# A staged transformer kernel on one core: three seams reordered (opening transposes, expert queries, closing stage)

## The reference

```python
h = x @ w_in                                   # projections of 256 tokens
...
x = _layernorm(DEEPNORM_ALPHA * x + (o * jax.nn.silu(gate)) @ w_out, ln_g[i], ln_b[i])
```

```python
x = x + gate1[:, None, :] * (merged @ w_out[l])
h2 = modulate(x, norm_ffn_g[l], shift2, scale2)
# peer_ffn: queries, two sets of 128 sub-keys, top 16 of 256 pairs, then two tables of 16384 rows
q = (hf @ w_q).reshape(T, PEER_HEADS, 2, PEER_HALF)
s = jnp.einsum('thpd,hpnd->thpn', q, sub_keys)
a = jax.nn.gelu(jnp.einsum('cd,chkd->chk', x_c, u), approximate=False)
y = jnp.einsum('chk,chkd->cd', g_c * a, vv)
x = x + gate2[:, None, :] * y
return rmsnorm(x, norm_final_g)
```

## Time and profile before

| | us |
|---|---|
| median of three runs | 1747.11 |
| the profiled execution | 1730.18 |
| its span, first to last instruction | 1728.4 |
| TensorE busy in it | 1615.2 |
| VectorE busy | 1180.4 |
| ScalarE busy | 865.2 |

### The profile page before, as it was taken

How to read it: one execution, slowest core, us unless ns; L and a number is a source line. 1 busy time by engine, 2 the same in 40 slices (tenths; PEclk the granted TensorE clock), 3 DMA queues, 4 the chain that set the end, 5 groups by cost and what they waited for, 6 DMA issues and landing times.

```text
span 1728.4 us, 31280 instructions
## 1 busy us (share of the span) xinstructions
PE 1615.2 (93%) x10766; PEld 1392.1 (81%) x10766; DVE 1180.4 (68%) x2504; ACT 865.2 (50%) x1391; POOL 81.1 (5%) x110
## 2 busy tenths in 40 slices
PE   5889999998998889998999999899999999999996
PEld 4667877896677667776899999899999777778885
DVE  3565656755576666546347999788787999975554
ACT  3564544444556644453235666655655444445553
POOL 1030101100111210000000000000000000000000
PEclk9999989999998989999689999999999999999998
DMA  6544544555555447534244455544444454566552
GB/s 219 174 147 146 195 147 134 189 172 182 175 194 190 163 141 246 164 102 146 97 145 133 162 193 168 172 159 157 157 158 146 159 167 160 166 207 193 192 192 81
DMA packets 77188, 284.83 MB, mean 165 GB/s; under 512 B 9376, under 2 KB 9408, under 8 KB 75840
## 3 DMA queue, kind: packets, MB, share of 16 engines
q1 hardware_dynamic: 73296, 266.95, 46.5%
q0 software_dynamic: 3824, 16.99, 2.9%
HBM read 281.77 MB, written 2.14 MB: 164 GB/s over the span
## 4 chain that ended last, share of the span: by engine, by line
PE 74%; DVE 16%; ACT 4%; issue 3%; DMA 3%; DVEq 0%; SPq 0%; POOL 0%; ACTq 0%
PE banks L639 21%; PE banks L641 20%; PE banks L640 20%; DVE w_lo L1372 5%; PE banks L1027 3%; PE banks L774 2%; DMA raw<-stream 2%; PE banks L811 2%; PE banks L729 2%; PE banks L751 1%; DMA arena<-x_spill 1%; PE banks L823 1%; PE banks L822 1%; DVE arena L1841 1%; ACT w_hi L1085 1%
## 5 line engine op out<-in xcount | busy, mean ns | idle before, releaser
L1372 DVE TENSOR_TENSOR w_lo<-raw,w_hi 128x1024 fp32r<-128x1024 f32 x456 | 558.4, 1229 | 343.1 <-ACT w_hi L1085 338.5
L1085 ACT ACTIVATE w_hi<-raw 128x1024 fp32r<-128x1024 f32 x456 | 481.7, 1058 | 520.2 <-PE banks L641 478.5
L639 PE MATMUL banks<-w_hi,xT_hi 128*128 128x512 f32 (+1 forms) x1140 | 453.8, 398 | 14.9 <-DVE xT_lo L1406 6.0
L641 PE MATMUL banks<-w_hi,xT_lo 128*128 128x512 f32 (+1 forms) x1140 | 442.8, 388 | 0.0
L640 PE MATMUL banks<-w_lo,xT_hi 128*128 128x512 f32 (+1 forms) x1140 | 442.6, 388 | 0.0
L639 PE MATMUL banks<-xT_hi,w_hi 128*128 128x256 f32 (+1 forms) x1392 | 409.2, 294 | 4.9 <-DVE xT_lo L1406 2.9
L640 PE MATMUL banks<-xT_lo,w_hi 128*128 128x256 f32 (+1 forms) x1392 | 403.6, 290 | 0.0
L641 PE MATMUL banks<-xT_hi,w_lo 128*128 128x256 f32 (+1 forms) x1392 | 403.5, 290 | 0.0
L639 PEld LDWEIGHTS banks<-xT_hi,w_hi 128*128 128x128 f32 x1392 | 277.4, 199 | 6.0 <-DVE xT_lo L1406 3.1
L640 PEld LDWEIGHTS banks<-xT_lo,w_hi 128*128 128x128 f32 x1392 | 277.4, 199 | 0.1
L641 PEld LDWEIGHTS banks<-xT_hi,w_lo 128*128 128x128 f32 x1392 | 277.0, 199 | 0.0
(11 more groups left out here) (189 smaller groups left out, 1445.8 us busy)
## 6 DMA issues: line engine op xcount, KB each, us to landing
raw<-stream SPq DMA_DIRECT2D x504, 512.0 KB, 3.6
arena<-ln_in POOLq DMA_DIRECT2D x4, 1024.0 KB, 5.3
arena<-x_spill POOLq DMA_DIRECT2D x3, 1024.0 KB, 10.9
arena<-mod_rows POOLq DMA_DIRECT2D x2, 1536.0 KB, 9.7
arena<-g_in POOLq DMA_DIRECT2D x3, 512.0 KB, 10.6
arena<-x_in SPq DMA_DIRECT2D x2, 512.0 KB, 4.0
arena<-bands_in POOLq DMA_DIRECT2D x1, 1024.0 KB, 6.7
arena<-keys_in POOLq DMA_DIRECT2D x1, 1024.0 KB, 6.1
```

The costliest lines, as they stand in the source:

```text
L639: pe.matmul(out, stationary[0], moving[0], start=first, stop=False, **k)
L641: return pe.matmul(out, stationary[1], moving[0], start=False, stop=last, **k)
L1085: act.activation(w_hi[:, s], half_raw(s), ACT.Copy).then_inc(piece_hi, 1)
L1372: dve.tensor_tensor(w_lo[:, s], half_raw(s), w_hi[:, s].bitcast(F32), ALU.subtract).then_inc(piece_lo, 1)
```

## The change

It has four parts. At the opening, the turned halves don't wait for one another's banks, ScalarE and VectorE evacuate them ahead of the four splits, and TensorE turns both blocks before the first product. The form of the product that takes a feature unit one block at a time goes away. The expert queries wait for both blocks and go through `project` from the first unit on; VectorE modulates block 1 one split earlier and evacuates its turned halves one split earlier. At the end, the last four pieces are multiplied for block 0 first and then for block 1, and each engine closes one block at a time, with the table for the root loaded ahead.

```diff
-                    after = (earlier[half],) if earlier else (closing[0],) if closing else ()
+                    after = (earlier[half],) if earlier else (closing[0],) if closing else (None,)
...
-            def project_opening(unit, turned, turn_other):
+            def project_opening(unit, turned, turn_other=None):
...
-                        if b == 0 and n == RING - 1:
+                        if b == 0 and n == RING - 1 and turn_other is not None:
                             turn_other()
...
-                turn_block(0)
-                project_opening(unit, turned, lambda: turn_block(1))
+                for b in range(B):
+                    turn_block(b)
+                project_opening(unit, turned)
...
-            open_layer(E["q"][0], E["hT"], h_half, 4, peer["h"])
-            for u in E["q"][1:]:
+            for n, u in enumerate(E["hT"]):
+                pe.wait_ge(h_half, 4 + n + 1)
+                turn(u, peer["h"])
+            wait_put(pe, E["hT"])
+            for u in E["q"]:
                 project(u)
...
-            with pe.Fori(0, HALF // RING) as i:
+            with pe.Fori(0, HALF // RING - 1) as i:
                 for s in range(RING):
                     second_table(RING * i + HALF, s)
+            for b in range(B):
+                for s in range(RING):
+                    if b == 0:
+                        pe.wait_ge(piece_lo, n_pieces - RING + s + 1)
+                        pe.wait_ge(hidden_lo, NKEYS - RING + s + 1)
+                    for d in range(D // COLS):
+                        mm = parts_product(banks[:, 2 * b + d], [x[:, s, b * P:(b + 1) * P] for x in (xT_hi, xT_lo)],
+                                           [x[:, s, d * COLS:(d + 1) * COLS] for x in (w_hi, w_lo)],
+                                           False, False, skip_group_check=True)
+                    if b:
+                        mm.then_inc(piece_used, 1)
+                if b == 0:
+                    mm.then_inc(first_block, 1)
...
                 if l == 0:
-                    split_ahead(0)
                     for u in L["xT"]:
                         evacuate_only(u)
+                    split_ahead(0)
...
-            act.wait_ge(x_ready, 2)
+            root_table()
             for b in range(B):
+                act.wait_ge(end_ready, b + 1)
                 link(act.activation(y_end[:, b], x_end[:, b], ACT.Square, accum_out=small[:, 8 + b:9 + b]))
-            act.activation(small[:, 0:B], small[:, 8:8 + B], ACT.Sqrt, bias=small[:, 5:6], scale=1.0 / D).then_inc(dev_ready, 1)
+                act.activation(small[:, b:b + 1], small[:, 8 + b:9 + b], ACT.Sqrt, bias=small[:, 5:6], scale=1.0 / D).then_inc(dev_ready, 1)
...
             for u in E["hT"][0:2]:
                 evacuate_only(u)
+            pieces_behind(out, 2)
+            modulate_block(peer["h"], moba["mod"][:, 4], moba["mod"][:, 3], 1)
             pieces_behind(out, 3)
-            modulate_block(peer["h"], moba["mod"][:, 4], moba["mod"][:, 3], 1)
-            pieces_behind(out, RING)
             for u in E["hT"][2:4]:
                 evacuate_only(u)
+            pieces_behind(out, RING)
...
-            dve.wait_ge(piece_used, n_pieces)
             dve.wait_ge(end_loaded, 48)
...
+            dve.wait_ge(first_block, 1)
+            close_end(0)
+            norm_end(0)
+            dve.wait_ge(piece_used, n_pieces)
+            close_end(1)
+            norm_end(1)
```

More of the change, by code:

```diff
@@ L436, in build @@
         rms_ready, stored = sem("rms_ready"), sem("stored")
+        first_block, end_ready = sem("first_block"), sem("end_ready")
         evac_sem = {"act": evac_act, "dve": evac_dve}
@@ L678, in block_products @@
                 x = [part[:, k, block * P:(block + 1) * P] for part in (xT_hi, xT_lo)]
-                if unit.kind == "token":
-                    return parts_product(bank[0][:, 0:unit.cols], x, [part[:, kt, 0:unit.cols] for part in w], first, last,
-                                         skip_group_check=True)
-                for t in range(4):
-                    at = (t % 2) * S + block * P
-                    mm = parts_product(bank[t // 2][:, at:at + P], [part[:, kt, t * P:(t + 1) * P] for part in w], x,
-                                       first and t % 2 == 0 and block == 0, last, skip_group_check=True)
-                return mm
+                return parts_product(bank[:, 0:unit.cols], x, [part[:, kt, 0:unit.cols] for part in w], first, last,
+                                     skip_group_check=True)
             def project_closing(units):
@@ L694, in project_closing @@
                         for kt in range(PK):
-                            mm = block_products(unit, b, [bank_of(unit, 0)], w, PK * n + kt, kt)
+                            mm = block_products(unit, b, bank_of(unit, 0), w, PK * n + kt, kt)
                         if b:
@@ L707, in project_opening @@
                             wait_put(pe, [turned[2 * b + n // 2]])
-                        if b == 0 and n == RING - 1:
+                        if b == 0 and n == RING - 1 and turn_other is not None:
                             turn_other()
                         w = take_piece(n if b == 0 else 0)
-                        bank = [bank_of(unit, b)] if unit.kind == "token" else [bank_of(unit, 0), bank_of(unit, 1)]
                         for kt in range(PK):
-                            mm = block_products(unit, b, bank, w, PK * n + kt, kt)
+                            mm = block_products(unit, b, bank_of(unit, b), w, PK * n + kt, kt)
                         if b:
@@ L1946, in _, with close_end, norm_end @@
                     rest_of_hidden(RING * i + HALF + RING, s)
-            dve.wait_ge(piece_used, n_pieces)
             dve.wait_ge(end_loaded, 48)
-            for b in range(B):
+            def close_end(b):
                 flat = banks[:, 2 * b:2 * b + 2].rearrange("p q n -> p (q n)")
                 link(dve.tensor_tensor(y_end[:, b], flat, gate2, ALU.mult))
-                link(dve.tensor_tensor(x_end[:, b], x_end[:, b], y_end[:, b], ALU.add))
-            dve.sem_inc(x_ready, 1)
-            inverse_root(small[:, 0:B], small[:, 2:4])
-            for b in range(B):
+                dve.tensor_tensor(x_end[:, b], x_end[:, b], y_end[:, b], ALU.add).then_inc(end_ready, 1)
+            def norm_end(b):
+                inverse_root(small[:, b:b + 1], small[:, 2 + b:3 + b])
+                dve.wait_ge(end_ready, b + 1)
                 dve.scalar_tensor_tensor(out=y_end[:, b], in0=x_end[:, b], scalar=small[:, 2 + b:3 + b], in1=final_gain,
                                          op0=ALU.mult, op1=ALU.mult).then_inc(rms_ready, 1)
+            dve.wait_ge(first_block, 1)
[4 more added lines that the diff above has]
+            norm_end(1)
 def lay_out(a):
```

## The result

| | before | after |
|---|---|---|
| median of the comparison's four executions, us | 1746.16 (1744.22 to 1751.63) | 1699.0 (1693.3 to 1708.17) |
| ratio of after to before | | 0.973, 95% interval 0.9674 to 0.9786 |
| profiled execution, us | 1730.18 | 1703.83 |
| its span, us, and mean granted clock | 1728.4, 0.961 | 1702.0, 0.963 |

The change makes the kernel 2.7% faster. The forecast was 1707.0 us with a range of 1700 to 1723. The two profiled executions differ by only 26.4 us, the medians by 47. Both differences need an explanation.

What follows compares the result with a forecast made beforehand. TensorE, busy 93% of the span, was taken as the bound, with gains only where it waits, runs slowly or has finished. Opening 10.0, seam 24.0 and end 6.1 sum to 40.1 us: 1747.1 - 40.1 = 1707.0 us, range 1700 to 1723.

Steps and rivals of the forecast that it cites:

- Opening: Start of the kernel: turning both blocks early and evacuating before the splits brings work 10.0 us earlier, ends 7 and 11.
- Seam: Entry to the expert queries: 96 matmuls of 256 columns replace 192 of 128, 24.0 us earlier, ends 20 and 26.
- 13.6 is the halved count at the old price: At the expert seam: 13.6 of the 24.0 us come from halving the matmuls, the rest from the clock returning sooner.
- lost overlap: At the expert seam: TensorE stands still while block 1 is normalised, so the first query product comes 6.9 us later.
- End: Closing stage: block 0 closes beside block 1's matmuls, so the kernel ends 6.1 us earlier, ends 4.5 and 7.6.
- straight code behind TensorE's loop: Ahead of the last matmuls: a possible pause of 1.4 us that would cut the closing gain to 4.5 us.
- rival A: Expert seam: low clock lasts some 47 us whatever is multiplied; seam gains 8.8 us, total 1722 us; chance 0.08.
- B: Expert seam: unprofiled runs lack the low-clock stretch; seam gains 3 us, total 1728 us; chance 0.05.
- D: Behind the expert seam: the clock falls and does not rise on 256 columns; slower, 1884 us; chance 0.02.
- 2.5 us of scatter of a median on either side: Whole kernel: allowance of 2.5 us for a median's scatter, added at both ends of the forecast range.
- the sum's far end, 1702.5: Whole kernel: the time if all three parts reach their upper gains, 11 + 26 + 7.6 = 44.6 us.
- the base: Whole kernel: the median of the kernel before, 1747.1 us, from which the summed gain of 40.1 us was taken.

Runs made afterwards that it cites:

- e1_open: The kernel before with only the change's opening (both blocks turned ahead of the splits); median 1736.47 us against 1746.53.
- e6_turned: The kernel before with both blocks turned at once, the four splits still ahead of the evacuations; median 1742.65 us against 1746.5.
- e3_end: The kernel before with only the change's closing stage, closed block by block; median 1738.39 us against 1746.53.
- e4_all: The kernel after, unchanged, run again beside its parts on one chip; median 1704.02 us against 1746.53 for the kernel before.
- e2_query: The kernel before with only the change's expert seam (both blocks turned, then four query units of 256 columns); median 1721.03 us against 1746.53.
- e9_warm128: The kernel before with six matmuls of zeros in TensorE's idle time at the expert seam; median 1724.92 us against 1746.5.
- e8_warm: The kernel after with 14 and 4 matmuls of zeros in its idle time at the expert seam; median 1705.06 us, kernel before 1746.5.
- e7: The kernel before with only the root's table load moved ahead of the last wait; 1754.81 us in a single execution against 1751.78.
- e5_form: The kernel after with the first query unit again as 192 matmuls of 128 columns; median 1732.66 us, kernel before 1746.5.
- e11_again: The kernel after once more, for its scatter, on another chip; median 1701.75 us, kernel before 1751.78.
- e10_warmall: The kernel after with matmuls of zeros in TensorE's idle time at twelve places; median 1679.75 us, kernel before 1751.78.

## Why the prediction was wrong by a little, and where it was right

**Opening: right in the profile, by two errors of some 1.4 us that cancel.** 10.0 us forecast, 9.9 in the profile and 10.7 (good to 2.2) by the means of e1_open. That the profile gives 9.9 is luck. The first product was forecast for 13.2 and came at 13.12. The second unit was forecast for 25.9 and came at 27.43: all twelve matmuls ahead of the third piece ran at half clock, 0.427 apart, where I took seven (five times 0.2, 1.0 us), and the third piece was ready at 19.17, not at 17.6, since the stream landed at 16.71. In before it was 15.31, in e1_open 15.13, in e6_turned 16.37 and in e3_end 17.28, so this differs from one execution to the next. The other error is in the reading of before: "block 1's products start at 30.39, the second unit at 35.94". Block 1 is turned ahead of block 0's last piece, so the matmuls at 30.39 are that piece's six, and the second unit starts six matmuls later than I took, at 37.3 (the copy at 37.50 says so). For pieces 5 to 8 the stream is not late: ScalarE waits for TensorE there.

**Seam, right in size and wrong in its reason.** 24.0 us forecast; 23.2 in the profile, 24.6 in e4_all's (64.39 less 39.77), 24.8 (good to 1.8) by the means of e2_query. First query product forecast for 14.9 us behind the square (838.5 less 823.58), measured 15.2; 21 matmuls at half clock forecast, some 28 measured, and the transposes took 1.97 us for 1.93. The step "13.6 is the halved count at the old price (96 x 0.214 = 20.5, less the 6.9 of lost overlap); the rest is the clock" is where the reason failed, though it did not move the sum: the old price, 0.214, was itself the low clock. At full clock the old unit takes 192 x 0.112 = 21.5 us (e9_warm128) and the new one 96 x 0.120 = 11.5, so the halved count is worth 10.0 and the lost overlap costs 6.9. Form and order together are worth 3 to 4 us at full clock (4.1 between e9_warm128 and e8_warm), and the other 19 to 20 are the clock. The sum came out right because both shares were counted at what they cost. But the share given to the halved count, 13.6, is some four times what the form is worth at full clock, and a reader who took the reason would have halved matmuls where 2.75 us of filler gives nearly as much.

**End, right.** 6.1 us forecast, 6.4 in the profile (14.9 to 8.5), 6.3 in e3_end's. The straight code behind TensorE's loop costs no pause; block 1 was held up by 0.1 us, as forecast. Last matmul to end was forecast as 8.8 and is 8.5.

**The page on the clock.** The kernels before, e1, e3, e6 and e7 each kept the stretch of 47.8 us at the seam in which TensorE is busy nearly throughout, and e5_form kept 51.2. The Trainium skill, TensorE: Matmul & The Clock Gate, Part 1, says that sustained activity alone releases the throttle. The trace disagrees for these 128-column fp32r matmuls and agrees for the 256-column ones, which brought 1.00 back after 5.9 us. So rival A falls: it had the low clock last some 47 us whatever is multiplied, and with the new form it lasted 10.2 to 13.7. B falls as well: each profile of a kernel with the old seam has the stretch, and an e9_warm128 that gains 22 us by the medians would have gained nothing if unprofiled executions had no such stretch. D, the slower side, did not happen: 256 columns brought the clock back in every kernel here, 2 to 6 us after the first of them.

**The failed step: the scatter, beside an opening taken too small.** The range was made "with 2.5 us of scatter of a median on either side", and its lower end is the sum's far end, 1702.5, less that term. Three executions of before within 6.4 us of one another were all that I took it from. Over 16 executions of the kernel after (the four, e4_all and e11_again) the mean is 1701.3 and the standard deviation 5.5 us; over 55 of before 1746.4 and 5.4. A median of four then scatters by some 3.0 us (1.09 x 5.5 / 2, one standard deviation), so the value that was to be forecast can lie some 6 us to either side where I allowed 2.5. The median over all sixteen is 1702.6, inside the range; the four gave 1699.0. And I had the sign in hand: "the profiled 1730.18, which stands 16.9 us (1.0%) under the median" says that two executions of one kernel can differ by 1%, and I used it only to choose the base of the sum.

Most of the scatter is time at half clock. In the profiles these are stretches of 3 to 34 us in the attention of two layers, different in each execution. The record also has the mean granted clock of each execution, and from it follows the time at 0.50: twice what the mean lacks to 1.00, times the span. Over the 51 executions of before that ran beside the experiments it is 171 us on average, and an execution is longer by 0.39 us for each us of it (correlation 0.96); what is left scatters by only 1.7 us. So 0.01 of the mean clock goes with 14 us, not with the 8 that was expected for e4_all. The profiled execution of before has 135 us in this account, 36 fewer; at 0.39 that is 14 of the 16 us by which it lies under the mean. The same account shows the seam in unprofiled executions: e2_query has 138 us on average, 33 fewer than before, and its profile has 37.6 fewer at the seam.

**Where the 8.0 us between forecast and median are.** The parts sum to 40.1 us in the forecast and to 39.5 in the profiles above (9.9 + 23.2 + 6.4), but the means of all executions differ by 45.1, with a standard error of 1.6 (5.4 / 7.4 and 5.5 / 4, combined). Between the two profiled executions nothing is missing: apart from the seam they have 88.2 us at half clock before and 112.8 after, and half of those 24.6 us taken from 39.5 gives 27.2, where they differ by 26.4. The other profiles show that the opening is mis-sized. The copy that ends the first unit stands at 37.50 in before, but at 38.77 to 40.32 in the four other profiles with the old opening (e2, e3, e7, e9); the average of the five is 39.0, that of the seven with the new opening 27.6 (26.13 to 29.81). So the opening is worth 11.5 us, not 10.0, and 11.3 of them still stand where the first attention begins (241.58 in before, the same averages taken there). The stream is the reason: in the old order the first product starts 6.8 us behind the third piece's split in all five profiles, and that split starts at 15.31 in before and at 16.60 to 17.28 in the other four. With 24.4 us for the seam (64.6 on average in five profiles, 40.1 in four) and 6.3 for the end the parts sum to 42.2. So of the 8.0 us, 0.7 are the base (1747.1 for a mean of 1746.4), 2.1 the parts, the opening above all, and 2.3 the draw of four (1701.3 against 1699.0). The other 2.9 stay open; they are less than two standard errors.

## What to carry to other kernels

Look at the granted clock in the windows of a busy TensorE before counting its instructions: a stretch at 0.50 behind an idle time of 3 us cost this kernel more than the instructions that were taken out, and some matmuls of zeros in the idle time took it away. Where a kernel has such stretches, a single profiled execution can stand 1% off the median, so compare parts by landmarks inside the profile (from one fixed event to another) and whole kernels by ten executions or more. A range for a measured median needs the scatter of single executions in it, and three runs don't give that.

## What the runs showed of the hardware that was not expected

- In an idle time of 2.9 us (8 us around the transposes in e5_form) the granted clock fell to 0.50 and stayed there for 47.8 to 51.2 us under nearly unbroken fp32r matmuls with 128 moving columns (five kernels and e5_form); with 256 columns it was back 5.9 us after the first of them in the kernel after and 3 us in e2_query, e4_all and e11_again. The same 128-column matmuls keep 1.00 when they start at 1.00 (e9_warm128, 195 records in 22 us).
- In attention, with small fp32 matmuls, a low stretch lasted up to 34 us (e2_query, e5_form, e9_warm128), with TensorE busy for most of it (30.61 of 34.10 us in e2_query, 30.00 of 31 in e1_open), and its length differs from one execution to the next.
- An fp32r matmul with its weight load takes 0.112 us with 128 columns and 0.120 with 256 at full clock, and 0.213 with either at half clock. So at full clock 256 columns cost 7% more than 128, and at half clock the same.
- One matmul of fp32 zeros with 256 columns takes 0.46 us (2.75 us for six, two records each), and with such groups throughout the program the time at 1.2 GHz fell by 101 us (132.1 in e11_again, 31.0 in e10_warmall) and the kernel's median by 22.
